# Normalised rows kept in natural order in place of h, h rebuilt from them, two weight pieces asked for in another order

## The chip, the cores and the metric

One core of one Trainium2 chip. The metric is the device time of one execution of the kernel in microseconds (us), the median of several runs. Engines: TensorE (PE), VectorE (DVE), ScalarE (ACT), GpSimd (POOL) and SyncE (SP), which here only asks for DMA transfers.

## The reference

One encoder block over 512 tokens of width 1024, in f32. The parts that matter here:

```
h = h + concat([a, s]) @ w_out              # a: pooling mixer, s: state-space mixer
v = rmsnorm(h, g_ffn)
h = h + hierarchical_moe(v)                 # 4 groups x 8 experts; top-1 group, top-2 experts in it
gate = sigmoid(rmsnorm(h, g_ple) @ ple_gate_w + ple_gate_b)
h = h + gate * (p @ ple_proj_w)
out = rmsnorm(h, g_final)

# expert e, on its tokens: (silu(v @ w_gate[e]) * (v @ w_up[e])) @ w_down[e]
# w_gate, w_up: (1024, 256), w_down: (256, 1024): 3 MB an expert, 96 MB in all
```

Each token's result is the sum of two experts' rows with weights w1 and w2. A row's normalisation is a division by root = sqrt(mean(h^2) + eps), followed by the gain g_ffn on the columns.

## The kernel before

Each engine has a program of its own, written out by hand, and the engines meet at semaphores. The tokens are four tiles of 128 (t = 0 to 3; NT = 4, NA = 3); tile h holds them in SBUF, tokens on partitions, 1024 columns a tile.

Stages, in order: the mixers (to some 165 us); w_out's second half (wout1, eight blocks of 512 columns, on TensorE) whose results VectorE adds into h (residual); the norm and the router (165 to 219 us); 32 experts (to some 447 us); the tail, that is the combination, the gate, and the final norm.

The norm and the router. ScalarE takes the squares of a tile of h with their sum (mean_root) and the root; VectorE inverts the root in place (norm, column S_RS2); ScalarE's scaled_rows multiplies h by it and writes zbuf. It does that in another column order: chunk j of a row (128 columns) gets the columns 8p + j, since w_gate and w_up are loaded with row 8p + j on partition p. TensorE transposes h itself for the router (turned), and VectorE and TensorE make the logits. GpSimd stores each tile of h to h_d and each tile of zbuf to v_d in DRAM. For the first expert pair nothing is gathered: TensorE picks the rows of experts 0 and 1 out of zbuf by matmuls with 0/1 matrices (picked, two groups of tiles: 0 and 1, then 2 and 3, once VectorE's mask of the last tile is there).

The experts. Slots are 64 tokens an expert; for each later pair GpSimd gathers 128 rows of v_d into moe (rows_in), TensorE transposes them in 8 chunks (x_rows, line 1935), VectorE applies the gain and writes them back (x_out). For each expert TensorE does gate and up (32 passes of 256 columns, gate_up), a transpose (h_rows, line 1954), and down (8 passes of 512 columns). ScalarE copies the result out, GpSimd scatters it to pairs_d.

Weights come in pieces of 1 MB: piece p = 3e + k is gate, up or down (k = 0, 1, 2) of expert e. 22 buffers hold them: 12 in ring (0 to 11), 4 in big (12 to 15), 2 in zbuf (16, 17), 2 in h (18, 19), 2 in ut (20, 21). SP asks for the first 22 in an order written by hand, each group behind the wait that says that its buffer is free; from piece 22 on each takes the buffer of piece AFTER[p] once the experts have used it (gu_ps counts gate_up, dn_ps down). So h must be stored before its buffers take pieces 18 and 19, and it is loaded back before the tail (line 498).

The tail. VectorE adds to each tile of h the two gathered rows of pairs_d times the weights S_W1 and S_W2 (combine), then the last two experts' share from a PSUM bank.

Every matmul here goes through L1586, every recorded tensor_tensor of VectorE through L855, every activation copy through L531, every weight request through L356.

Of the kernel before, what the change touches and what calls it, by code (L numbers as in the profile page):

```python
# [26 lines left out]
ALU = mybir.AluOpType  # L27
# [5 lines left out]
P = 128  # L33
# [100 lines left out]
def build(nc, A, out):  # L134
    ctx = ExitStack()
    with ctx:
# [6 lines left out]
        def scratch(name, shape, dt=F32):  # L143
# [32 lines left out]
        S_SS, S_RS, S_EPS, S_W1, S_W2, S_SS2, S_RS2, S_SS3, S_RS3, S_SS4, S_RS4, S_HALF, S_WARM = (  # L176
            0, 4, 8, 12, 16, 20, 24, 28, 32, 36, 40, 44, 45)
        S_A2, S_T1, S_T2 = 64, 64 + 4 * G, 64 + 6 * G
        S_S30 = S_A2
# [45 lines left out]
        v_d = scratch("v_d", [T, DM])  # L225
        h_d = scratch("h_d", [T, DM])
        tbl_d = scratch("tbl_d", [T * NE, 1], I32)
# [9 lines left out]
        down_ready = [sem(f"down_ready{k}") for k in range(LOADS)]  # L237
        h_stored, h_back = sem("h_stored"), sem("h_back")
        half_in, x1_done = sem("half_in"), sem("x1_done")
# [125 lines left out]
        def _(sp):  # L365
# [82 lines left out]
            for p in range(6, 12):  # L448
                weights(sp, p)
            sp.wait_ge(wo1_ps, 2 * NT)  # L450
            for p in (14, 15, 21):
                weights(sp, p)
            sp.wait_ge(turned_ps, KC + 1 + NT)
            sp.wait_ge(h_stored, 16 * NT)
            sp.wait_ge(v_done, NT)
            for p in (18, 19):
                weights(sp, p)
            sp.wait_ge(v_stored, 16 * NT)
            sp.wait_ge(xT_ps, 2)
            for p in (16, 17):  # L460
                weights(sp, p)
# [30 lines left out]
            def load_pairs(t):  # L492
# [5 lines left out]
            sp.dma_start(at(h, ALL, 0, [[DM, NT], [1, DM]]),  # L498
                         dr(h_d, 0, [[DM, P], [P * DM, NT], [1, DM]])).then_inc(h_back, 16)
            sp.wait_ge(gu_ps, NE - 1)  # L500
# [27 lines left out]
        def _(act):  # L528
# [188 lines left out]
            def scaled_rows(t):  # L717

                act.wait_ge(rstd_done, NT + t + 1)
                act.activation(at(zbuf, ALL, t * DM, [[1, P], [P, KC]]), at(h, ALL, t * DM, [[KC, P], [1, KC]]),  # L720
                               ACT.Copy, scale=at(small, ALL, S_RS2 + t, [[1, 1]])).then_inc(v_done, 1)

            for t in range(NA):
                act.wait_ge(h_done, 2 * (t + 1))
                mean_root(at(h, ALL, t * DM, [[1, DM]]), at(zbuf, ALL, t * DM, [[1, DM]]), S_SS2, t, ss_done)
                act.wait_ge(ss_done, NT + t + 1)
                act.activation(at(small, ALL, S_RS2 + t, [[1, 1]]), at(small, ALL, S_SS2 + t, [[1, 1]]), ACT.Sqrt,
                               bias=at(small, ALL, S_EPS, [[1, 1]]), scale=1.0 / DM).then_inc(rms_root, 1)
                scaled_rows(t)
            t = NA  # L730
            act.wait_ge(h_done, 2 * NT - 1)
            mean_root(at(h, ALL, t * DM, [[1, 512]]), at(zbuf, ALL, t * DM, [[1, 512]]), S_HALF, 0, half_in)
            act.wait_ge(h_done, 2 * NT)
            mean_root(at(h, ALL, t * DM + 512, [[1, 512]]), at(zbuf, ALL, t * DM + 512, [[1, 512]]), S_SS2, t, ss_done)
            act.wait_ge(ss_done, 2 * NT)
            act.wait_ge(half_root, 1)
            act.activation(at(small, ALL, S_RS2 + t, [[1, 1]]), at(small, ALL, S_SS2 + t, [[1, 1]]), ACT.Sqrt,
                           bias=at(small, ALL, S_HALF, [[1, 1]]), scale=1.0 / DM).then_inc(rms_root, 1)
# [112 lines left out]
        def _(dve):  # L851
# [211 lines left out]
            def norm(t):  # L1063
                inverse(S_RS2 + t, 1, NT + 1 + t)

# [214 lines left out]
            def weights_and_slots():  # L1280
# [6 lines left out]
                seq(tt(at(small, ALL, S_W1, one), qv("gp", one), qv("dn", one), ALU.mult))  # L1287
                seq(tt(at(small, ALL, S_W2, one), at(small, ALL, S_W1, one), qv("ex", one), ALU.mult))
                for i, x in enumerate((NE - 2, NE - 1)):
                    for k, col in ((1, S_W1), (2, S_W2)):  # L1290
                        own.do(tt(qv("wb", one, (k - 1) * NT), qv(f"M{k}", [[NE, NT]], x), at(small, ALL, col, one), ALU.mult))
                    own.settle()
                    own.do(tt(qv("wt", one, i * NT), qv("wb", one), qv("wb", one, NT), ALU.add))
                    seq(pick(qv(f"X{x}", [[P, NT], [1, P]]), cv(C_PLACE, [[0, NT], [1, P]]), 1.0,
                             qv(f"rk{x}", [[1, NT], [0, P]]), ALU.add, ALU.is_equal))
                    tt(qv(f"X{x}", [[P, NT], [1, P]]), qv(f"X{x}", [[P, NT], [1, P]]), qv("wt", [[1, NT], [0, P]], i * NT),
                       ALU.mult).then_inc(x1_done, 1)
# [33 lines left out]
            def combine(t):  # L1331
                dve.wait_ge(ld_pairs[t], 16)
                if t == 0:
                    dve.wait_ge(h_back, 16)
                for n in range(2):
                    hv = at(h, ALL, t * DM + n * 512, [[1, 512]])
                    for k, col in enumerate((S_W1, S_W2)):
                        dve.scalar_tensor_tensor(hv, at(big, ALL, t * 2 * DM + k * DM + n * 512, [[1, 512]]),
                                                 at(small, ALL, col + t, [[1, 1]]), hv, ALU.mult, ALU.add
                                                 ).then_inc(comb, 1)  # L1340
                        if k == 0:
                            dve.wait_ge(comb, 6 * t + 2 * n + 1)
                for n in range(2):
                    hv = at(h, ALL, t * DM + n * 512, [[1, 512]])
                    dve.wait_ge(cmb_ps, 2 * t + n + 1)
                    dve.wait_ge(comb, 6 * t + 4)
                    tt(hv, bank[2 * t + n][:, :], hv, ALU.add).then_inc(comb, 1)

# [59 lines left out]
        def _(pool):  # L1408
# [82 lines left out]
            for t in range(NT):  # L1491
                pool.wait_ge(h_done, 2 * (t + 1))
                pool.dma_start(dr(h_d, t * P * DM, [[DM, P], [1, DM]]), at(h, ALL, t * DM, [[1, DM]])
                               ).then_inc(h_stored, 16)
                pool.wait_ge(v_done, t + 1)
                pool.dma_start(dr(v_d, t * P * DM, [[DM, P], [1, DM]]), at(zbuf, ALL, t * DM, [[1, DM]])
                               ).then_inc(v_stored, 16)
# [86 lines left out]
        def _(pe):  # L1584
# [270 lines left out]
            def picked(t):  # L1855
# [3 lines left out]
                for j in range(KC):  # L1859
                    got = mm(bank[j // 4 * 6][:, (j % 4) * P:(j % 4 + 1) * P], at(zbuf, ALL, t * DM + j * P, [[1, P]]),  # L1860
                             at(moe, ALL, Q["X1"] + t * P, [[1, P]]), t == 0 and j % 4 == 0, t == NA, True)
# [71 lines left out]
            def x_rows(k):  # L1933
                for j in range(KC):
                    last = pe.transpose(bank[j // 4 * 6][:, (j % 4) * P:(j % 4 + 1) * P],  # L1935
                                        at(moe, ALL, M_XG + k * DM + j * P, [[1, P]]), ident)
                    if j % 4 == 3:
# [151 lines left out]
```

## Time and profile before

| what | value |
|---|---|
| median of 3 runs | 523.9 us (522.33 to 526.2) |
| span of the profiled execution | 522.6 us |
| the profiled execution's own time | the page gives the span alone |
| TensorE busy | 484.2 us (93%) |
| VectorE, ScalarE, GpSimd busy | 238.9, 163.6, 161.0 us |
| HBM read, written | 138.17 MB, 16.29 MB |
| chain that ended last | PE 70%, DMA 18%, DVE 3%, ACT 3%, SP's queue 3% |

The shares of busy time are averages over stages with different limits; the chain and the stretches say what limits which stage. Times in rows are us from the start of the span, unless marked ns.

### The profile page before, as it was taken

The numbers are of one execution on the slowest core, as the hardware profiler recorded it, in microseconds if no ns is written. First come the engines' busy times: TensorE is split into PE (matmuls) and PEld (weight loads), VectorE is DVE, ScalarE is ACT, GpSimd is POOL, SyncE is SP. The second block draws the span as 40 slices with busy tenths as digits, with TensorE's granted clock in tenths as the row PEclk, the third lists the DMA queues.
The fourth block names the chain that finished last, engine by engine and source line by source line (L and its number), as shares of the span: only waits on it lengthen the run. The fifth ranks groups of instructions, "written<-read, shape, count | busy, mean of one in ns | idle before, by whom it ended". The sixth has DMA issues, their size and how long they took to land.

```text
span 522.6 us, 7298 instructions
## 1 busy us (share of the span) xinstructions
PE 484.2 (93%) x2744; PEld 273.3 (52%) x2744; DVE 238.9 (46%) x683; ACT 163.6 (31%) x265; POOL 161.0 (31%) x144
## 2 busy tenths in 40 slices
PE   3799999999999998999999999779999998899993
PEld 3446776634854476765555554435454544444441
DVE  2899987999233347653222222102211211474524
ACT  5643335456442344111111111002212121313464
POOL 1069999944100111132222222202120210003350
PEclk9999999999999989999999999879999998999998
DMA  8874200499289965999999999999999997970012
GB/s 298 141 204 88 62 0 2 159 129 208 108 360 422 415 249 192 407 412 423 418 415 419 417 419 409 423 416 421 418 420 420 419 409 296 345 312 0 0 80 80
DMA packets 57083, 146.83 MB, mean 281 GB/s; under 512 B 27602, under 2 KB 32758, under 8 KB 44248
## 3 DMA queue, kind: packets, MB, share of 16 engines
q1 hardware_dynamic: 50872, 133.92, 69.0%
q0 software_dynamic: 5904, 12.41, 6.1%
q8 instruction: 22, 0.36, 0.3%
q14 instruction: 13, 0.11, 0.1%
q10 hardware_dynamic: 272, 0.04, 0.0%
HBM read 138.17 MB, written 16.29 MB: 296 GB/s over the span
## 4 chain that ended last, share of the span: by engine, by line
PE 70%; DMA 18%; DVE 3%; ACT 3%; SPq 3%; issue 1%; DVEq 0%
PE bank L1586 65%; DMA h<-in_exp_w_up_dram 11%; DMA big<-in_exp_w_up_dram 6%; SPq L356 3%; DMA h<-in_x_dram 1%; PE bank L1935 1%; PE bank L1677 1%; PE bank L1954 1%; ACT L539 1%; ACT moe L531 1%; PE bank L1821 1%; PE bank L2052 1%; DVE ring L855 1%; DVE moe L1092 1%; DVE moe L855 1%
## 5 line engine op out<-in xcount | busy, mean ns | idle before, releaser
L1586 PE MATMUL bank<-ring,moe 128*64 128x256 f32 (+3 forms) x976 | 127.3, 385 | 3.4 <-DMA ring<-in_exp_w_up_dram 3.0
L1586 PEld LDWEIGHTS bank<-ring,moe 128*64 128x64 f32 (+1 forms) x976 | 76.2, 144 | 38.2 <-issue 15.3
L1512 POOL DMA_INDIRECT pairs_d<-moe,sidx_all x32 | 32.0, 1000 | 159.8 <-PE bank L1935 83.0
L855 DVE TENSOR_TENSOR vrow<-moe,bank 64x128 f32<-64x128 f32 x64 | 18.6, 291 | 125.5 <-ACT moe L754 120.6
L1586 PE MATMUL bank<-big,ut 128*128 128x512 f32 x128 | 58.2, 609 | 1.2 <-ACT ut L676 1.2
L1586 PE MATMUL bank<-ut,big 128*128 128x512 f32 x128 | 57.3, 596 | 1.8 <-ACT ut L543 1.8
L754 ACT ACTIVATE moe<-bank 64x256 f32<-64x256 f32 x32 | 12.1, 378 | 143.3 <-PE bank L1586 143.3
L1586 PE MATMUL bank<-ring,ut 128*128 128x512 f32 x128 | 55.7, 593 | 0.4 <-DVE ut L855 0.4
L531 ACT ACTIVATE moe<-bank 128x512 f32<-128x512 f32 x56 | 32.6, 598 | 59.8 <-PE bank L1586 49.3
L1586 PE MATMUL bank<-big,moe 128*64 128x256 f32 (+1 forms) x264 | 44.9, 455 | 6.6 <-DMA big<-in_exp_w_up_dram 5.7
L1586 PEld LDWEIGHTS bank<-big,ut 128*128 128x128 f32 x128 | 24.6, 196 | 32.0 <-issue 31.7
L855 DVE TENSOR_TENSOR ring<-ring,bank 128x64 f32<-128x64 f32 (+1 forms) x142 | 39.5, 278 | 2.8
L1586 PEld LDWEIGHTS bank<-ring,ut 128*128 128x128 f32 x128 | 24.0, 190 | 29.3 <-issue 29.3
L1586 PEld LDWEIGHTS bank<-ut,big 128*128 128x128 f32 x128 | 23.4, 190 | 27.2 <-issue 26.6
L855 DVE TENSOR_TENSOR bank<-bank,ring 128x64 f32<-128x64 f32 (+1 forms) x142 | 35.2, 288 | 2.9
L1586 PEld LDWEIGHTS bank<-big,moe 128*64 128x64 f32 x264 | 22.5, 148 | 22.3 <-issue 7.6
L1586 PE MATMUL bank<-ring 128*64 128x128 f32 (+1 forms) x128 | 32.5, 437 | 0.0
L1272 DVE COPY moe<-bank 128x128 f32<-128x128 f32 x32 | 9.3, 292 | 44.9 <-PE bank L1954 44.8
L855 DVE TENSOR_TENSOR moe<-bank,vec 128x512 f32<-128x512 f32 x40 | 26.0, 687 | 5.5 <-PE bank L1935 3.5
L1580 POOL TENSOR_TENSOR ring<-ring,zbuf 128x512 f32<-128x512 f32 x6 | 8.7, 1444 | 47.7 <-ACT ring L816 47.7
L1586 PE MATMUL bank<-h,moe 128*64 128x256 f32 (+1 forms) x120 | 19.5, 454 | 4.1 <-DMA h<-in_exp_w_up_dram 4.1
L1586 PEld LDWEIGHTS bank<-ring 128*64 128x64 f32 (+1 forms) x128 | 15.2, 163 | 15.3 <-issue 15.0
(193 smaller groups left out, 600.5 us busy)
## 6 DMA issues: line engine op xcount, KB each, us to landing
ring<-in_exp_w_up_dram SPq DMA_DIRECT2D x19, 1024.0 KB
ring<-in_exp_w_down_dram SPq DMA_DIRECT2D x18, 1024.0 KB
ring<-in_exp_w_gate_dram SPq DMA_DIRECT2D x17, 1024.0 KB
big<-in_exp_w_gate_dram SPq DMA_DIRECT2D x7, 1024.0 KB
big<-in_exp_w_down_dram SPq DMA_DIRECT2D x7, 1024.0 KB
big<-in_exp_w_up_dram SPq DMA_DIRECT2D x6, 1024.0 KB
ut<-in_exp_w_gate_dram SPq DMA_DIRECT2D x4, 1024.0 KB
h<-in_exp_w_up_dram SPq DMA_DIRECT2D x4, 1024.0 KB
```

The costliest lines, as they stand in the source:

```text
L356: eng.dma_start(at(to[0], ALL, to[1], [[1, PIECE]]), w[e].rearrange("(p j) f -> p (j f)", p=P)).then_inc(done, 16)
L531: act.activation(o, i, ACT.Copy).then_inc(signal, 1)
L539: act.activation(at(small, ALL, S_WARM + k, [[1, 1]]), at(small, ALL, S_EPS, [[1, 1]]), function)
L754: act.activation(at(moe, (0, CAP), M_SG, [[1, DE]]), at(bank[1 + e % 2], (0, CAP), 0, [[1, DE]]), ACT.Silu).then_inc(sg_sb, 1)
L855: return dve.tensor_tensor(o, a, b, op)
L1092: return dve.scalar_tensor_tensor(o, a, b, c, op0, op1)
L1272: dve.tensor_copy(at(moe, ALL, M_HT + (e % 2) * P, [[1, P]]), bank[3][:, 0:P]).then_inc(hT_sb, 1)
L1512: pool.indirect_dma_start(pairs, bass.IndirectOffsetOnAxis(ap=index, axis=0), at(moe, ALL, M_Y + k * 512, [[1, 512]]), None, bounds_check= ...
L1580: seq(pool.tensor_tensor(sg, sg, at(zbuf, ALL, n * 512, [[1, 512]]), ALU.mult))
L1586: return pe.matmul(o, a, b, start=start, stop=stop, skip_group_check=loose)
L1677: last = pe.transpose(bank[B_WT + ri][:, (g % 4) * P:(g % 4 + 1) * P], rv(R_W + ri * 1024 + g * P, P), ident)
L1821: rows = pe.transpose(bank[H_BANK[t] + n][:, (j % 4) * P:(j % 4 + 1) * P], at(h, ALL, t * DM + j * P, [[1, P]]), ident)
```

## The change

The normalised rows are no longer written to zbuf but over h, in natural column order. TensorE then reads them with a step: the picks take columns j, j + 8, j + 16 ... of h, and x_rows does the same with the gathered rows. ScalarE therefore waits, ahead of each scaling, until TensorE has transposed that tile of h. h is not stored; the reload at line 498 takes v_d, and the combination works in normalised units: the roots are kept in S_ROOT2 beside the inverses, two new products S_V hold w1 and w2 times the inverse, and the last step of a tile multiplies by the root while it adds the bank. The squares' unused output goes to moe. SP asks for pieces 16 and 17 (zbuf) straight behind the ring's; 18 and 19 (h) take the place at which 16 and 17 stood, behind v_stored and xT_ps (the last pick).

```diff
--- before.py
+++ after.py
@@ -175,6 +175,7 @@
 
         S_SS, S_RS, S_EPS, S_W1, S_W2, S_SS2, S_RS2, S_SS3, S_RS3, S_SS4, S_RS4, S_HALF, S_WARM = (
             0, 4, 8, 12, 16, 20, 24, 28, 32, 36, 40, 44, 45)
+        S_ROOT2, S_V = 52, 56
         S_A2, S_T1, S_T2 = 64, 64 + 4 * G, 64 + 6 * G
         S_S30 = S_A2
 
@@ -223,7 +224,6 @@
         z_d = scratch("z_d", [P, G * NCH])
         k_d = scratch("k_d", [G * CH, 15 * CH])
         v_d = scratch("v_d", [T, DM])
-        h_d = scratch("h_d", [T, DM])
         tbl_d = scratch("tbl_d", [T * NE, 1], I32)
         pairs_d = scratch("pairs_d", [4 * T, DM // 2])
 
@@ -235,7 +235,7 @@
             sem(n) for n in ("ld_wout0", "ld_wlow", "ld_wout1", "ld_glu", "ld_ppw", "ld_wple", "ld_fin"))
         gu_ready = [sem(f"gu_ready{k}") for k in range(LOADS)]
         down_ready = [sem(f"down_ready{k}") for k in range(LOADS)]
-        h_stored, h_back = sem("h_stored"), sem("h_back")
+        h_back, vw_done = sem("h_back"), sem("vw_done")
         half_in, x1_done = sem("half_in"), sem("x1_done")
         cmb_ps = sem("cmb_ps")
         dve_step, pool_step = sem("dve_step"), sem("pool_step")
@@ -447,17 +447,14 @@
             sp.wait_ge(cat_done, NB)
             for p in range(6, 12):
                 weights(sp, p)
+            for p in (16, 17):
+                weights(sp, p)
             sp.wait_ge(wo1_ps, 2 * NT)
             for p in (14, 15, 21):
                 weights(sp, p)
-            sp.wait_ge(turned_ps, KC + 1 + NT)
-            sp.wait_ge(h_stored, 16 * NT)
-            sp.wait_ge(v_done, NT)
-            for p in (18, 19):
-                weights(sp, p)
             sp.wait_ge(v_stored, 16 * NT)
             sp.wait_ge(xT_ps, 2)
-            for p in (16, 17):
+            for p in (18, 19):
                 weights(sp, p)
             for p in range(NPIECE, 3 * NE):
                 e, k = AFTER[p] // 3, AFTER[p] % 3
@@ -496,7 +493,7 @@
 
             sp.wait_ge(gu_ps, NE - 5)
             sp.dma_start(at(h, ALL, 0, [[DM, NT], [1, DM]]),
-                         dr(h_d, 0, [[DM, P], [P * DM, NT], [1, DM]])).then_inc(h_back, 16)
+                         dr(v_d, 0, [[DM, P], [P * DM, NT], [1, DM]])).then_inc(h_back, 16)
             sp.wait_ge(gu_ps, NE - 1)
             load_gate(0, 0, 4, ld_wple)
             sp.wait_ge(moe_done, 1)
@@ -717,24 +714,25 @@
             def scaled_rows(t):
 
                 act.wait_ge(rstd_done, NT + t + 1)
-                act.activation(at(zbuf, ALL, t * DM, [[1, P], [P, KC]]), at(h, ALL, t * DM, [[KC, P], [1, KC]]),
-                               ACT.Copy, scale=at(small, ALL, S_RS2 + t, [[1, 1]])).then_inc(v_done, 1)
+                act.wait_ge(turned_ps, KC + t + 1 + (t == NA))
+                hv = at(h, ALL, t * DM, [[1, DM]])
+                act.activation(hv, hv, ACT.Copy, scale=at(small, ALL, S_RS2 + t, [[1, 1]])).then_inc(v_done, 1)
 
             for t in range(NA):
                 act.wait_ge(h_done, 2 * (t + 1))
-                mean_root(at(h, ALL, t * DM, [[1, DM]]), at(zbuf, ALL, t * DM, [[1, DM]]), S_SS2, t, ss_done)
+                mean_root(at(h, ALL, t * DM, [[1, DM]]), at(moe, ALL, M_XT, [[1, DM]]), S_SS2, t, ss_done)
                 act.wait_ge(ss_done, NT + t + 1)
-                act.activation(at(small, ALL, S_RS2 + t, [[1, 1]]), at(small, ALL, S_SS2 + t, [[1, 1]]), ACT.Sqrt,
+                act.activation(at(small, ALL, S_ROOT2 + t, [[1, 1]]), at(small, ALL, S_SS2 + t, [[1, 1]]), ACT.Sqrt,
                                bias=at(small, ALL, S_EPS, [[1, 1]]), scale=1.0 / DM).then_inc(rms_root, 1)
                 scaled_rows(t)
             t = NA
             act.wait_ge(h_done, 2 * NT - 1)
-            mean_root(at(h, ALL, t * DM, [[1, 512]]), at(zbuf, ALL, t * DM, [[1, 512]]), S_HALF, 0, half_in)
+            mean_root(at(h, ALL, t * DM, [[1, 512]]), at(moe, ALL, M_XT, [[1, 512]]), S_HALF, 0, half_in)
             act.wait_ge(h_done, 2 * NT)
-            mean_root(at(h, ALL, t * DM + 512, [[1, 512]]), at(zbuf, ALL, t * DM + 512, [[1, 512]]), S_SS2, t, ss_done)
+            mean_root(at(h, ALL, t * DM + 512, [[1, 512]]), at(moe, ALL, M_XT + 512, [[1, 512]]), S_SS2, t, ss_done)
             act.wait_ge(ss_done, 2 * NT)
             act.wait_ge(half_root, 1)
-            act.activation(at(small, ALL, S_RS2 + t, [[1, 1]]), at(small, ALL, S_SS2 + t, [[1, 1]]), ACT.Sqrt,
+            act.activation(at(small, ALL, S_ROOT2 + t, [[1, 1]]), at(small, ALL, S_SS2 + t, [[1, 1]]), ACT.Sqrt,
                            bias=at(small, ALL, S_HALF, [[1, 1]]), scale=1.0 / DM).then_inc(rms_root, 1)
             scaled_rows(t)
 
@@ -1061,7 +1059,10 @@
                 tt(hv, bank[n][:, :], hv, ALU.add).then_inc(h_done, 1)
 
             def norm(t):
-                inverse(S_RS2 + t, 1, NT + 1 + t)
+                dve.wait_ge(rms_root, NT + 1 + t)
+                dve.reciprocal(at(small, ALL, S_RS2 + t, [[1, 1]]), at(small, ALL, S_ROOT2 + t, [[1, 1]])
+                               ).then_inc(rstd_done, 1)
+                dve.wait_ge(rstd_done, NT + 1 + t)
 
             def turned(t):
 
@@ -1286,6 +1287,9 @@
                 seq(dve.reciprocal(qv("dn", one), qv("dn", one)))
                 seq(tt(at(small, ALL, S_W1, one), qv("gp", one), qv("dn", one), ALU.mult))
                 seq(tt(at(small, ALL, S_W2, one), at(small, ALL, S_W1, one), qv("ex", one), ALU.mult))
+                for k, col in enumerate((S_W1, S_W2)):
+                    tt(at(small, ALL, S_V + k * NT, one), at(small, ALL, col, one), at(small, ALL, S_RS2, one), ALU.mult
+                       ).then_inc(vw_done, 1)
                 for i, x in enumerate((NE - 2, NE - 1)):
                     for k, col in ((1, S_W1), (2, S_W2)):
                         own.do(tt(qv("wb", one, (k - 1) * NT), qv(f"M{k}", [[NE, NT]], x), at(small, ALL, col, one), ALU.mult))
@@ -1332,9 +1336,10 @@
                 dve.wait_ge(ld_pairs[t], 16)
                 if t == 0:
                     dve.wait_ge(h_back, 16)
+                    dve.wait_ge(vw_done, 2)
                 for n in range(2):
                     hv = at(h, ALL, t * DM + n * 512, [[1, 512]])
-                    for k, col in enumerate((S_W1, S_W2)):
+                    for k, col in enumerate((S_V, S_V + NT)):
                         dve.scalar_tensor_tensor(hv, at(big, ALL, t * 2 * DM + k * DM + n * 512, [[1, 512]]),
                                                  at(small, ALL, col + t, [[1, 1]]), hv, ALU.mult, ALU.add
                                                  ).then_inc(comb, 1)
@@ -1344,7 +1349,8 @@
                     hv = at(h, ALL, t * DM + n * 512, [[1, 512]])
                     dve.wait_ge(cmb_ps, 2 * t + n + 1)
                     dve.wait_ge(comb, 6 * t + 4)
-                    tt(hv, bank[2 * t + n][:, :], hv, ALU.add).then_inc(comb, 1)
+                    dve.scalar_tensor_tensor(hv, hv, at(small, ALL, S_ROOT2 + t, [[1, 1]]), bank[2 * t + n][:, :],
+                                             ALU.mult, ALU.add).then_inc(comb, 1)
 
             def turned_g_ple(t):
                 for n in range(2):
@@ -1489,11 +1495,8 @@
             pool.wait_ge(wo0_done, 2 * NT)
 
             for t in range(NT):
-                pool.wait_ge(h_done, 2 * (t + 1))
-                pool.dma_start(dr(h_d, t * P * DM, [[DM, P], [1, DM]]), at(h, ALL, t * DM, [[1, DM]])
-                               ).then_inc(h_stored, 16)
                 pool.wait_ge(v_done, t + 1)
-                pool.dma_start(dr(v_d, t * P * DM, [[DM, P], [1, DM]]), at(zbuf, ALL, t * DM, [[1, DM]])
+                pool.dma_start(dr(v_d, t * P * DM, [[DM, P], [1, DM]]), at(h, ALL, t * DM, [[1, DM]])
                                ).then_inc(v_stored, 16)
             pool.wait_ge(log_ps, NT)
             own.do(pool.memset(at(moe, ALL, M_XG + DM, [[1, DM]]), 0.0))
@@ -1857,7 +1860,7 @@
                 pe.wait_ge(x1_done, 1 if t < NA else 2)
                 pe.wait_ge(v_done, t + 1)
                 for j in range(KC):
-                    got = mm(bank[j // 4 * 6][:, (j % 4) * P:(j % 4 + 1) * P], at(zbuf, ALL, t * DM + j * P, [[1, P]]),
+                    got = mm(bank[j // 4 * 6][:, (j % 4) * P:(j % 4 + 1) * P], at(h, ALL, t * DM + j, [[KC, P]]),
                              at(moe, ALL, Q["X1"] + t * P, [[1, P]]), t == 0 and j % 4 == 0, t == NA, True)
                     if t == NA and j % 4 == 3:
                         got.then_inc(xT_ps, 1)
@@ -1933,7 +1936,7 @@
             def x_rows(k):
                 for j in range(KC):
                     last = pe.transpose(bank[j // 4 * 6][:, (j % 4) * P:(j % 4 + 1) * P],
-                                        at(moe, ALL, M_XG + k * DM + j * P, [[1, P]]), ident)
+                                        at(moe, ALL, M_XG + k * DM + j, [[KC, P]]), ident)
                     if j % 4 == 3:
                         last.then_inc(xT_ps, 1)
 
```

## Rows read from the trace of the kernel before

**Rows 1.** The profile's page: the span.

```profile
span 522.6 us, 7298 instructions
```

**Rows 2.** Stretches: busy us (x instructions) by engine, granted clock, DMA share, GB/s.

```profile
core 0: us, PE busy (x) PEld busy (x) DVE busy (x) ACT busy (x) POOL busy (x), PEclk, DMA share, GB/s
...
185.00:200.70 15.70, 15.70 (x83) 10.83 (x82) 9.49 (x38) 6.12 (x7) 1.59 (x3) 0.89 0.38 153
...
219.20:226.00 6.80, 5.74 (x42) 3.08 (x43) 5.55 (x21) 0.74 (x2) 2.77 (x3) 1.00 1.01 419
...
234.10:322.00 87.90, 87.83 (x659) 49.08 (x661) 22.83 (x59) 14.27 (x29) 22.77 (x23) 1.00 1.02 417
322.00:437.70 115.70, 102.40 (x648) 52.47 (x644) 19.96 (x54) 20.03 (x39) 19.77 (x20) 0.96 1.01 416
```

**Rows 3.** TensorE's waits between 300 and 450: us in total, times, longest.

```profile
PE bank L1586 <- DMA big<-in_exp_w_up_dram: 5.7, 2, 3.4
PE bank L1586 <- DMA h<-in_exp_w_up_dram: 4.1, 2, 3.4
```

**Rows 4.** The chain that ended last, 400 to 450: start us, us, what.

```profile
405.13 0.87 PE bank L1935 x8
...
406.37 31.25 DMA big<-in_exp_w_up_dram
...
437.66 7.01 PE bank L1586 x40
```

**Rows 5.** SP's timeline, first ask of each group: start us, us, what.

```profile
200.68 0.33 SPq L356 DMA_DIRECT2D big<-in_exp_w_down_dram  x1
...
211.52 0.33 SPq L356 DMA_DIRECT2D h<-in_exp_w_gate_dram  x1
...
214.15 0.33 SPq L356 DMA_DIRECT2D zbuf<-in_exp_w_up_dram  x1
...
219.18 0.33 SPq L356 DMA_DIRECT2D ring<-in_exp_w_up_dram  x1
...
225.95 0.33 SPq L356 DMA_DIRECT2D ring<-in_exp_w_gate_dram  x1
...
234.10 0.33 SPq L356 DMA_DIRECT2D ring<-in_exp_w_gate_dram  x1
```

**Rows 6.** The DMA queues between 200.6 and 226; GB/s in 40 slices of 0.635 us.

```profile
GB/s 0 103 155 374 374 387 284 284 303 348 355 426 432 400 394 452 426 439 400 374 323 374 400 400 400 400 413 413 452 400 426 413 439 426 426 406 419 400 445 413
...
q1 hardware_dynamic: 1106, 8.14, 81.2%
q0 software_dynamic: 411, 1.29, 12.5%
```

**Rows 7.** Groups of ScalarE by form: busy us, mean ns, idle before.

```profile
L720 ACT ACTIVATE zbuf<-h,small 128x1024 f32<-128x1024 f32 x4 | 8.3, 2083 | 11.8 <-DVE small L866 11.8
...
L535 ACT ACTIVATE zbuf<-h 128x1024 f32<-128x1024 f32 x3 | 3.2, 1053 | 5.4 <-DVE h L855 5.4
```

**Rows 8.** TensorE's timeline, 176 to 229: start us, us, what, idle before.

```profile
178.00 7.03 PE L1586 MATMUL bank<-big,ut 128*128 128x512 f32 x16
...
209.02 0.63 PE L1586 MATMUL bank<-moe,cst 128*128 128x32 f32 x4 [1.36 <-DVE moe L1092]
209.49 3.82 PE L1586 MATMUL bank<-moe,zbuf 128*128 128x128 f32 x32
```

**Rows 9.** VectorE's timeline: start us, us, what, idle before.

```profile
149.35 1.41 DVE L1050 SCALAR_TENSOR_TENSOR ring<-zbuf,vec,bank 128x512 f32<-128x512 f32 x2 [3.08 <-PE bank L1789]
...
222.05 0.23 DVE L855 TENSOR_TENSOR moe<-moe,small 128x4 f32<-128x4 f32 x2
...
453.61 1.29 DVE L855 TENSOR_TENSOR h<-bank,h 128x512 f32<-128x512 f32 x2
```

**Rows 10.** TensorE's operand loads by form: busy us, mean ns, idle before.

```profile
L1586 PEld LDWEIGHTS bank<-ring,moe 128*64 128x64 f32 x848 | 61.5, 137 | 37.2 <-issue 14.3 <-DMA ring<-in_exp_w_up_dram 3.5
...
L1935 PEld LDWEIGHTS bank<-cst,moe 128*128 128x128 f32 x120 | 13.4, 140 | 0.8 <-DMA moe<-v_d,gidx_all 0.8
...
L1586 PEld LDWEIGHTS bank<-rw,moe 128*128 128x128 f32 x64 | 7.4, 192 | 0.1
```

## The prediction

> **What bounds the kernel now.** First the span, 522.6 us [rows 1]. Then the stretches [rows 2]: between 185.0 and 200.7 us the DMA engines are busy for 0.38 of the time, and from 219.2 to 437.7 us for all of it, at 417 GB/s. TensorE is never idle in a way that matters before 322 us (87.83 of 87.90 us busy), but between 322 and 437.7 it works 102.40 of 115.70 us. So the experts have two phases: at first TensorE sets the pace and weights are ahead of it, later it has used up that lead and takes each weight as it lands. The waits [rows 3] say for what: weights, 5.7 us for those in big and 4.1 us for those in h alone. The chain that ended last [rows 4] shows the end of it: the last up-weights are asked for at 406.37, land at 437.66, and only then does the last expert start. A change in this kernel is therefore worth what it does to the landing of the last weights: when the DMA engines had nothing to move, and how much they must move in all. TensorE work is cheap as long as it fits into the 13.3 us (115.70 - 102.40) in which it waits.
>
> What can be asked for when is SP's list [rows 5]: three pieces at 200.68, the two pieces of h at 211.52 (line 454, behind the stores of h), the two pieces of zbuf at 214.15, when the picked rows are out of zbuf, two more at 219.18, three at 225.95, three at 234.10; each of the later ones waits until an expert has used its buffer.
>
> **The early pieces.** The change asks for the two zbuf pieces behind the ring's, that is at about 168 us. They then move while the DMA engines are two thirds idle: 2 x 1.0486 MB at 417 GB/s is 5.0 us, and the gap is 15.7 x (1 - 0.38) = 9.7 us wide. Nothing waits behind them on SP's queue but the wait for wout1. The fourth store of h (0.52 MB, 1.3 us), which lies in the busy stretch, goes too; the three before it lay in the gap and cost nothing. Naively the last weights would land 5.0 + 1.3 = 6.3 us sooner.
>
> **What is given back.** The pieces of h must now wait until the picked rows are out of h, as zbuf's did: 214.15 instead of 211.52. The three pieces of 200.68 (3.15 MB, 7.5 us) and the last store of rows (0.52 MB, 1.3 us) are moved by about 210.5 us, so the queue is empty for some 4.5 us before 215.2 (the first bytes come about 1.0 us after an ask, as the first slices of the queue's view show: 0 and 103 GB/s [rows 6]). Now the count that matters, at 226.0. Before: 9 pieces, 9.44 MB, were asked for since 200.6 and 8.14 MB of them moved [rows 6] (the tenth, of 225.95, has hardly begun), so 1.30 MB, 3.1 us, were outstanding. After: from 215.2 the pieces of h and those of 219.18, 4.19 MB, and the gathers' 0.24 MB (1.29 - 1.05 of queue 0, the 1.05 being the two stores of 0.52 MB each [rows 6]) take 4.43 / 0.417 = 10.6 us, to 225.8. The queue is then just empty, and the pieces of 225.95 begin at about 227.0. The lead is 3.1 us and 1.0 us of it is lost to that start: 2.1 us. It can't be more, since no buffer is free sooner; between 227.0 and 235.1 three pieces and queue 0's share (3.15 + about 0.3 MB) fill 8.1 us x 0.417 = 3.4 MB, so no further gap opens. From there the DMA engines are full to the end, as before, and the lead reaches the last landing. Its bounds: 3.1 us if the start is hidden, 1 us if the slowest of the 16 engines, which decides a landing, was emptier than the mean. I take 2.3 us, a little over the count, since part of the gathers' bytes moves after 226.
>
> **Small terms.** ScalarE's scaling of the rows takes 2083 ns with both sides stepped and should take what a contiguous pass over h takes, 1053 ns [rows 7]: 1.0 us less, four times. None of it is on the path: the last two picks wait for VectorE's mask (1.36 us idle before 209.02 [rows 8]). ScalarE's new wait for TensorE's transposes costs nothing by the order on TensorE, where the transposes of a tile precede its scaling in all four tiles; behind it stand only ScalarE's next squares and root. If that cover were missing, the last tile would carry it to the picks, less than 1 us. VectorE gets two products of 4 columns between the weights and the slot matrices: two such take 0.23 us [rows 9] at 222 us, where a delay only releases buffers 0.1 to 0.2 us later. In the tail the add of bank and h becomes a multiply and add of the same operands: 1.29 us for two adds against 1.41 us for two instructions of that kind that read a bank [rows 9], so 0.12 us a tile, of which one or two tiles lie on the path. The reload of h moves the same 2 MB. Together 0.3 us lost at most.
>
> **The stepped reads.** TensorE now reads h and the gathered rows with a step of 8 elements, 32 bytes, always as the operand that it loads: in the 120 transposes of gathered rows (15 groups of 8, 0.87 us each [rows 4]) and in the 64 passes of the picks (3.82 us for 32 [rows 8]). No row shows a stepped operand on TensorE, so I bound it. A load of 128 columns takes 192 ns in a matmul, one of 64 takes 137, so a column costs 0.86 ns and the rest is a fixed 82; in a transpose 128 columns take 140 ns [rows 10], 0.45 ns each. The pace of the transposes, 0.87 / 8 = 109 ns, is then that of the other operand's 128 columns (16 passes of 512 columns in 7.03 us [rows 8], 0.86 ns a column), not of the load. So the read of a loaded operand can run at 0.45 ns, and if a step halves that rate, it is 0.9: the transposes stay at 109 to 116 ns and the picks at 119. That is the lower bound, 0 to 0.8 us in all. A gain is excluded, the same columns are loaded. The middle is a doubling of the picks' 0.86, to 1.7 ns: 213 ns a load, +104 x 120 = 12.5 us for the transposes, and +3.2 us for each 32 passes of the picks, of which 1.36 us were idle: 5.0 us. The upper bound is what ScalarE pays, 2.03 ns an element (2083 / 1024) [rows 7]: 260 ns a load, 18.1 us for the transposes and 4.5 us for each 32 passes, 7.6 us with the idle time taken off. I take the lower bound, since the row nearest to it is of the same engine and the same operand.
>
> The Trainium skill has a rule that speaks against the change (Advanced Engine Details and Errata, SBUF Cachelines): a line of SBUF is 16 bytes, and with a different line for each access there is a penalty. ScalarE's rows agree, 2083 against 1053 ns [rows 7]; that it reaches TensorE's loads no row shows. If it doubles their time, the result is that of the second case below, if the load hides it, that of the first.
>
> **The cases.** The profiled span is 522.6 us, 1.3 us under the median of the three runs, and the page gives no other time of that execution; I apply the differences to the median, 523.9. A measurement of this kernel can tell about 1%, 5.2 us, from no change.
> 1. The forecast: loads hide the steps, lead 2.3 us: 521.6. Chance 0.50.
> 2. Slower: the steps double the loads. The ask for the h pieces and the release of every later buffer come 5.0 us later, and the lead of 2.1 us pays a part: +3 us. TensorE's own sum, 12.5 + 5.0 = 17.5 us, just fits into its 13.3 us of waits and the 0.04 x 115.7 = 4.6 us that the lowered clock costs it between 322 and 437.7 [rows 2]; I add 0.3: 527.2. It decides as soon as each group of picks grows by more than 1.5 us. For it: ScalarE's stepped rows. Against: the transposes' loads, twice as fast as they need be. Chance 0.28.
> 3. Slower still: the loads cost what ScalarE pays. 18.1 + 7.6 = 25.7 us against 17.9: TensorE sets the end, +8, 532. Chance 0.07.
> 4. The naive sum counts in full, the queue doesn't run dry: -6.3 us, 517.6. Against it: buffers are released only at 219 and 226 us. Chance 0.07.
> 5. The removed stores and early pieces only shift the gap: 523.9. Chance 0.08.
>
> The range takes in cases 1, 2 and 5 with their bounds, 518.2 to 528.2, and leaves out 3 and 4 (0.14). Faster by over 1% (under 518.7): case 4 and a corner of 1, 0.09. Slower by over 1% (over 529.1): case 3 and the upper end of 2, 0.11. Within: 0.80.
>
> **What would show it.** The DMA share between 185 and 200.7 rises from 0.38 to about 0.7. A new gap stands between about 210.5 and 215.2, and the queue is thin at 226. The groups of eight stepped transposes take 0.87 us and the 32 passes 3.82: this tells cases 1, 2 and 3 apart at a glance. TensorE's waits between 322 and 437 stay near 13 us; the last up-weights land at about 435.4, and from there to the end it is 84.9 us as before. The prediction is wrong if the picks grow, if the queue is dry for more than about 1 us after 219, or if the tail changes length, for instance because the clock falls elsewhere: the last expert's 7.01 us [rows 4] stand in a stretch whose granted clock is below full.

## The result and the profile after

The changed kernel takes 528.11 us (median of 4, 527.24 to 530.38) against 524.52 us for the kernel before on the same chip: ratio 1.0087, 95% interval 1.0052 to 1.0123. By the ratio that is 4.6 us more (2.7 to 6.5), where 2.3 us less was forecast. The profiled execution took 530.38 us, its span is 528.3 us, 5.7 us over the span before [rows 1].

The prediction named the rows to look at first: the picks (the matmuls that take the rows of experts 0 and 1 out of h) and the transposes of the gathered rows. TensorE's timeline of the changed kernel (start us, us, what):

```profile
178.53 7.03 PE L1589 MATMUL bank<-big,ut 128*128 128x512 f32 x16
...
204.37 7.86 PE L1589 MATMUL bank<-moe,h 128*128 128x128 f32 x32
212.06 0.53 PE L1589 MATMUL bank<-moe,cst 128*128 128x32 f32 x4
212.43 7.86 PE L1589 MATMUL bank<-moe,h 128*128 128x128 f32 x32
```

The first row is where it was, 0.53 us later. SP's asks at 144.14 and 144.67 us already differ by as much, so this part of the difference between the two spans arose before anything that was changed, and it is taken off below. Each group of 32 passes takes 7.86 us in place of 3.82 [rows 8], and no idle time is left between the groups. TensorE's loads by form follow: those of the picks in the kernel before, then those of the picks and of the transposes in the changed kernel. The last fence has rows of the chain that ended last (400 to 460 us).

```profile
L1586 PEld LDWEIGHTS bank<-moe,zbuf 128*128 128x128 f32 x64 | 7.3, 192 | 0.0
```

```profile
L1589 PEld LDWEIGHTS bank<-moe,h 128*128 128x128 f32 x64 | 15.4, 335 | 0.0
...
L1938 PEld LDWEIGHTS bank<-cst,moe 128*128 128x128 f32 x120 | 14.5, 190 | 0.7 <-DMA moe<-v_d,gidx_all 0.7
```

```profile
411.89 0.89 PE bank L1938 x8
...
412.93 30.32 DMA big<-in_exp_w_up_dram
...
443.30 7.08 PE bank L1589 x40
```

```profile
168.71 1.07 SPq L356 DMA_DIRECT2D zbuf<-in_exp_w_up_dram  x1
...
201.20 0.33 SPq L356 DMA_DIRECT2D big<-in_exp_w_down_dram  x1
...
220.39 0.33 SPq L356 DMA_DIRECT2D h<-in_exp_w_gate_dram  x1
...
226.16 0.33 SPq L356 DMA_DIRECT2D ring<-in_exp_w_up_dram  x1
...
232.93 0.33 SPq L356 DMA_DIRECT2D ring<-in_exp_w_gate_dram  x1
```

```profile
185.00:200.70 15.70, 15.70 (x82) 11.00 (x81) 9.03 (x34) 4.35 (x7) 1.08 (x2) 0.89 0.48 197
...
214.20:219.20 5.00, 5.00 (x23) 5.00 (x22) 1.35 (x4) 0.92 (x2) 0.00 (x0) 1.00 0.00 0
...
322.00:437.70 115.70, 105.17 (x680) 55.26 (x678) 21.25 (x56) 19.99 (x39) 20.85 (x21) 0.97 1.01 418
```

```profile
232.90:322.00 89.10, 88.43 (x663) 50.68 (x665) 24.31 (x67) 14.90 (x31) 24.16 (x25) 1.00 1.01 409
```

The zbuf pieces are early, as the change says. The h pieces are asked for at 220.39, while the kernel before reached the same place in the list at 214.15 [rows 5], and between 214.2 and 219.2 the DMA engines move nothing. The row of queue 1 between 200.6 and 232.9 us (packets, MB, share) says how the queue stands when the next three pieces are asked for:

```profile
q1 hardware_dynamic: 963, 7.10, 58.8%
```

Seven pieces, 7.34 MB, were asked for and 7.10 moved: 0.24 MB are left, where the kernel before had 1.30 MB at 226.0. The sum: that point comes 232.9 - 226.0 - 0.5 = 6.4 us later, and 1.06 MB more have moved by then, 2.5 us of work at 417 GB/s. That leaves 3.9 us. The last up-weights land 443.30 - 437.66 - 0.53 = 5.1 us later, so another 1.2 us were lost behind that point. The prediction put about 1.0 us on the start of the next pieces into an empty queue; the rate behind it is lower, 409 GB/s from 232.9 to 322 against 417 [rows 2], but how the 1.2 us divide is not shown. From the landing to the end it is 85.0 us, before 84.9.

### The profile page after: what moved, and what is told of

Read it like the earlier page. It is cut to its first block, busy times and chain, and to the rows that moved or that the text cites. A ratio compares the mean times of both kernels' runs of the same rounds, so it can differ in the third digit from the quotient of the medians.

```text
span 528.3 us, 7299 instructions
## 1 busy us (share of the span) xinstructions
PE 491.6 (93%) x2744; PEld 281.5 (53%) x2744; DVE 238.6 (45%) x685; ACT 159.9 (30%) x265; POOL 157.7 (30%) x140
## 4 chain that ended last, share of the span: by engine, by line
PE 71%; DMA 20%; ACT 3%; DVE 2%; SPq 2%; issue 1%; DVEq 0%; POOL 0%; POOLq 0%
PE bank L1589 66%; DMA big<-in_exp_w_up_dram 6%; DMA h<-in_exp_w_up_dram 6%; DMA ring<-in_exp_w_up_dram 5%; DMA moe<-v_d,gidx_all 2%; SPq L356 2%; PE bank L1938 1%; DMA h<-in_x_dram 1%; PE bank L1680 1%; ACT moe L528 1%; PE bank L1957 1%; ACT L536 1%; PE bank L1824 1%; PE bank L2055 1%; DVE moe L853 0%
## 5 line engine op out<-in xcount | busy, mean ns | idle before, releaser
L1589 PE MATMUL bank<-ut,big 128*128 128x512 f32 x128 | 59.1, 611 | 2.6 <-ACT ut L540 2.6
L1510 POOL DMA_INDIRECT moe<-v_d,gidx_all x15 | 15.6, 1042 | 23.5 <-DVE sidx_all L1242 18.8
L528 ACT ACTIVATE zbuf<-bank 128x512 f32<-128x512 f32 x16 | 11.5, 717 | 36.5 <-PE bank L1589 36.5
```

The lines of the kernel that those rows point to most:

```text
L528: act.activation(o, i, ACT.Copy).then_inc(signal, 1)
L1510: pool.indirect_dma_start(at(moe, ALL, M_XG + k * DM, [[1, DM]]), None, v_d, bass.IndirectOffsetOnAxis(ap=index, axis=0), bounds_check=T - ...
L1589: return pe.matmul(o, a, b, start=start, stop=stop, skip_group_check=loose)
```

## The experiments

In all of them ratios are to the kernel before, run on the same chip. Where experts compute on the wrong columns, the text under Expected says so: those kernels measure time and are no replacement.

**Picks without a step** (the changed kernel):

```
-  mm(..., at(h, ALL, t * DM + j, [[KC, P]]), at(moe, ALL, Q["X1"] + t * P, ...
+  mm(..., at(h, ALL, t * DM + j * P, [[1, P]]), at(moe, ALL, Q["X1"] + t * P, ...
```

> The changed kernel, with one thing altered: the picks read 128 adjacent columns of h instead of every eighth, so experts 0 and 1 compute on the wrong columns. Theory 1, the stepped loads of the picks are the whole loss: 32 passes take 3.8 us again instead of 7.9, the h pieces are asked for at about 214.5 instead of 220.4, and the time is 2 us below the kernel before (ratio 0.996), that is some 5 us below the changed kernel. Theory 2, the loss lies elsewhere (tail, gathers, order of the asks): the ratio stays between 1.005 and 1.012.

Measured 521.14 us, ratio 0.9962 (0.9945 to 0.9978). Its timeline and chain:

```profile
202.55 3.82 PE L1589 MATMUL bank<-moe,h 128*128 128x128 f32 x32
207.25 3.82 PE L1589 MATMUL bank<-moe,h 128*128 128x128 f32 x32
```

```profile
402.13 31.91 DMA big<-in_exp_w_up_dram
434.08 5.39 PE bank L1589 x40
```

The picks are back at 3.82 us and the whole loss is gone: the kernel is 2.0 us (1.2 to 2.9) faster than the one before. The second theory is out: the tail, the gathers and the list of asks cost too little together to cancel that gain. This is close to the 2.3 us that the prediction forecast with unslowed picks; the section on why it was wrong says by which route.

**Zbuf pieces late** (the changed kernel):

```
-  for p in (16, 17): weights(sp, p)        # behind the ring's
...
-  for p in (18, 19):
+  for p in (18, 19, 16, 17):
```

> The changed kernel, but the two zbuf pieces are asked for where the kernel before asked for them, behind the h pieces. Theory 1, the DMA engines have run dry by the time of the next asks at 233, so the early pieces save what the late ones would keep them busy with: the last up-weights land 5.0 us later less the 1 us of the dry spell that they fill, time 4 us above the changed kernel, ratio to the kernel before 1.016. Theory 2, early pieces are worth nothing because buffers set the pace: the time of the changed kernel, 1.008.

Measured 532.89 us, ratio 1.0172 (1.0144 to 1.0200): 0.85% or 4.5 us over the changed kernel's ratio, where 4 us were expected. The two intervals don't meet, so the early asks are worth something; by their widths the 4.5 us are good to some 2.3 us (an estimate), and the two traces say 3.1 (table below). In this kernel, without them the loss would have been larger, by the ratios about twice as large.

**Stepped picks in the kernel before:**

```
-  mm(..., at(zbuf, ALL, t * DM + j * P, [[1, P]]), ...
+  mm(..., at(zbuf, ALL, t * DM + j, [[KC, P]]), ...
```

> The kernel before, with one thing altered: the picks read every eighth column of zbuf, so experts 0 and 1 compute on the wrong columns. Theory 1: 32 passes take 7.9 us, zbuf pieces and every later buffer come 6.4 us later, while the h pieces are still asked for at 211.5; the DMA engines run dry for about 3 us before 221 and have no backlog at 233, as in the changed kernel, so the time is as much above the kernel before as the changed kernel's or a little more: ratio 1.009. Theory 2, the step matters only through h: 1.000 to 1.003.

Measured 529.14 us, ratio 1.0121 (1.0095 to 1.0146). The stretch in which the DMA engines starve:

```profile
215.00:221.00 6.00, 5.87 (x37) 4.89 (x36) 2.66 (x5) 0.00 (x0) 0.00 (x0) 1.00 0.63 233
```

The step alone, with everything else as before, costs 6.3 us (5.0 to 7.6), as much as the whole change or more (the intervals overlap, so which of the two is more stays open). The h pieces don't wait for the picks in this kernel and were asked for at 209.87. That didn't prevent the loss: the zbuf pieces and every later buffer still wait for the picks.

**The price by the size of the step.** The changed kernel with picks that read every second, third and fourth column; one execution each:

```
-  at(h, ALL, t * DM + j, [[KC, P]])
+  at(h, ALL, t * DM + j % 4 * P, [[2, P]])     # or 3, or 4
```

> The changed kernel, but the picks read every second column (8 bytes) of 256, so experts 0 and 1 compute on the wrong columns. Theory 1, a line of 16 bytes counts and two hits in a line are enough: 32 passes take 3.8 us, a load 192 ns. Theory 2, any step doubles a load: 7.9 us and 335 ns.

> The changed kernel, but the picks read every third column (12 bytes), so experts 0 and 1 compute on the wrong columns. Theory 1, a line of 16 bytes counts: 128 columns touch 96 lines, so the price is between: 32 passes take about 5.2 to 7.9 us. Theory 2, the price starts at 16 bytes: 3.8 us.

> The changed kernel, but the picks read every fourth column (16 bytes), so experts 0 and 1 compute on the wrong columns. Theory 1, one hit in a line: 32 passes take 7.9 us and a load 335 ns, as with a step of 8. Theory 2, the price grows with the distance: less than that.

The picks of the three, in that order, each its second group, and the mean of a load:

```profile
208.64 4.01 PE L1589 MATMUL bank<-moe,h 128*128 128x128 f32 x32
...
L1589 PEld LDWEIGHTS bank<-moe,h 128*128 128x128 f32 x64 | 7.7, 196 | 0.0
```

```profile
207.74 5.79 PE L1589 MATMUL bank<-moe,h 128*128 128x128 f32 x32
...
L1589 PEld LDWEIGHTS bank<-moe,h 128*128 128x128 f32 x64 | 11.3, 261 | 0.0
```

```profile
209.66 7.71 PE L1589 MATMUL bank<-moe,h 128*128 128x128 f32 x32
...
L1589 PEld LDWEIGHTS bank<-moe,h 128*128 128x128 f32 x64 | 15.1, 329 | 0.0
```

With steps of 1, 2, 3, 4 and 8 a group of 32 passes takes 3.82, 4.01, 5.79, 7.71 and 7.86 us. A step of two is nearly free, a step of four costs the full price, and eight costs no more than four. These executions took 522.56, 525.02 and 526.94 us beside 522.65 for the kernel before. The order is that of the picks, but they are single executions, and those of one kernel lie up to 4 us apart, so the price of a step is read from the passes and not from these times.

The Trainium skill has a rule (Advanced Engine Details and Errata, SBUF Cachelines): a line of 16 bytes, and at least two hits in it to hide the access. The traces agree with it on TensorE's loads too. At a step of two f32 every line gets two reads, 4.01 us; at four and eight each gets one, 7.71 and 7.86. At a step of three, 12 bytes, two of every four reads share a line and two are alone, so half of the price is due: 3.82 + (7.71 - 3.82) / 2 = 5.8 us, an estimate from that rule and the two rows; 5.79 was measured.

**Transposes without a step** (the changed kernel, picks still stepped):

```
-  at(moe, ALL, M_XG + k * DM + j, [[KC, P]]), ident)
+  at(moe, ALL, M_XG + k * DM + j * P, [[1, P]]), ident)
```

> The changed kernel, with one thing altered: the transposes of the gathered rows read 128 adjacent columns, so experts 2 to 31 compute on the wrong columns; the picks stay stepped. Theory 1, the transposes hide their slower loads behind the identity's stream and what little they cost lies in TensorE's waits: the time of the changed kernel within 0.5 us, ratio to the kernel before 1.008 to 1.010. Theory 2, their loads (190 ns in place of 140) cost 0.05 us each after all, 6 us in all: ratio 0.998 to 1.002.

Measured 529.06 us, ratio 1.0116 (1.0095 to 1.0136), not below the changed kernel's 1.0087 (1.0052 to 1.0123), and its loads take 141 ns. So the 120 stepped transposes cost nothing that can be measured: theory 1, though the ratio is above the window it gave, and the 0.998 to 1.002 of theory 2 is out. That they are paced by the identity's 128 columns, as the prediction had it, fits their 0.89 / 8 = 111 ns against 128 x 0.86 = 110; no run varied the identity.

**The kernel before without stores of h:**

```
-  pool.dma_start(dr(h_d, ...), at(h, ...)).then_inc(h_stored, 16)      # and the wait for it
-  dr(h_d, 0, ...)).then_inc(h_back, 16)
+  dr(v_d, 0, ...)).then_inc(h_back, 16)
```

> The kernel before without the four stores of h and without the wait for them; what is loaded back is the scaled rows, so the output misses h. Theory 1: of the four stores only the last lies in the busy stretch, so 0.52 MB fewer are moved there and the last weights land 1.3 us sooner: ratio 0.9975. Theory 2, buffers bound the asks and the queue is shorter at 226 but not empty: the same 1.3 us, no more, although the h pieces are asked for 5 us sooner. Theory 3, stores of GpSimd's queue cost nothing beside weights: 1.000.

Measured 521.99 us, ratio 0.9986 (0.9968 to 1.0005). The expected 0.9975 and no effect both lie in the interval, so this doesn't settle what a store is worth. The h pieces were asked for at 205.47 instead of 211.52, and even so the stores and these earlier asks together are worth 1.7 us at most: an ask put behind pieces that still keep the queue busy gained nothing that shows here.

**Plain picks by another layout of four pieces.** The loss can be avoided in a kernel that computes the right result. Only experts 0 and 1 are picked, and their gate and up weights can be loaded with the rows in natural order, so that their tokens are wanted in adjacent columns:

```
+  if natural:      # gate and up of experts 0 and 1
+      eng.dma_start(at(to[0], ALL, to[1], [[DE, KC], [1, DE]]),
+                    w[e].rearrange("(j p) f -> p j f", p=P)).then_inc(done, 16)
-  x_out(0, xT_sb, 2)
+  x_out(0, xT_sb, 2, V_FB)                      # g_ffn in natural chunks
-  at(h, ALL, t * DM + j, [[KC, P]])
+  at(h, ALL, t * DM + j * P, [[1, P]])
```

> The changed kernel without the stepped picks, by another layout for the two experts that are picked: gate and up of experts 0 and 1 are loaded with row 128 j + p on partition p, in runs of 1 KB in place of 8 KB, the picks read adjacent columns, and the gain of that pair is taken in the other order. It computes the reference. Theory 1: as with plain picks alone, 2 us below the kernel before, ratio 0.996, if the four pieces in 1 KB runs land by the first expert; their transfer lies between 145 and 165 us, and if it is slower it only fills the gap after 190. Theory 2, short runs are so slow that the ring's pieces are late: expert 0 waits for weights and the ratio is over 1.005.

Measured 521.50 us, ratio 0.9968 (0.9952 to 0.9984): 1.7 us faster than the kernel before and 6.2 us faster than the changed one, and every expert reads the right columns. Two of its stretches:

```profile
143.00:166.00 23.00, 23.00 (x99) 11.41 (x96) 7.86 (x9) 8.84 (x13) 1.27 (x1) 1.00 0.95 334
...
186.00:201.00 15.00, 15.00 (x91) 11.00 (x91) 10.52 (x38) 5.36 (x10) 1.08 (x2) 1.00 0.59 233
```

The four pieces in runs of 1 KB lie in the first stretch, and it is slower: 334 GB/s against 373 in the kernel before between 143 and 166 us. What is late by it only fills the gap behind (share 0.59 from 186 to 201, 0.33 before), and TensorE waits for none of it.

**And the first two tiles of h released early,** on top of that:

```
-  sp.wait_ge(v_stored, 16 * NT); sp.wait_ge(xT_ps, 2); weights(sp, 18); weights(sp, 19)
+  sp.wait_ge(v_first, 32); sp.wait_ge(x_zero, 2); weights(sp, 18)     # tiles 0 and 1 stored and picked
+  sp.wait_ge(v_stored, 32); sp.wait_ge(xT_ps, 2); weights(sp, 19)
```

> The kernel with plain picks and the other layout for experts 0 and 1, and piece 18 (tiles 0 and 1 of h) asked for as soon as the first two tiles are picked and stored, at about 208, piece 19 where it was. Theory 1, buffers bound the lead: the queue is empty at 226 either way, and the gap before 215 is only exchanged for one between 222 and 227; gain over the kernel without this 0 to 0.5 us, ratio to the kernel before 0.996. Theory 2, the gap counts in full: 2.5 us sooner, ratio 0.992.

Measured 521.94 us, ratio 0.9981 (0.9967 to 0.9995). Its stretches around the asks:

```profile
208.00:215.00 7.00, 6.85 (x58) 6.02 (x59) 5.32 (x21) 1.80 (x4) 0.00 (x0) 1.00 0.93 344
215.00:221.00 6.00, 4.88 (x43) 3.40 (x44) 2.51 (x13) 0.38 (x1) 2.29 (x3) 1.00 0.65 249
```

The gap before 215 is filled (share 0.93, without this 0.59) and stands after it instead (0.65, without this 0.95). No gain, as the first theory had it.

**All the traces, measured from the first pick.** The early part of a trace is up to 2.8 us shorter or longer, mostly with TensorE's clock (last section). From the start of the first pick to the start of the last expert's matmuls, which wait for the last up-weights, that part is left out (starts in us, from TensorE's timelines):

| kernel | first pick | last expert | between |
|---|---|---|---|
| before | 203.84 | 437.66 | 233.8 |
| before, stepped picks | 202.45 | 441.57 | 239.1 |
| before, no stores of h | 203.48 | 436.50 | 233.0 |
| changed | 204.37 | 443.30 | 238.9 |
| changed, zbuf pieces late | 204.58 | 446.59 | 242.0 |
| changed, plain transposes | 204.13 | 443.62 | 239.5 |
| changed, picks of step 4, 3, 2 | 201.75, 201.75, 203.94 | 440.55, 437.91, 436.18 | 238.8, 236.2, 232.2 |
| changed, plain picks | 202.55 | 434.08 | 231.5 |
| plain picks, other layout | 202.15 | 433.76 | 231.6 |
| the same, h released early | 203.85 | 436.43 | 232.6 |

These are single traces, but they agree with the ratios: with stepped picks of 8 both kernels are 5.1 to 5.3 us behind the kernel before, and with plain picks the change gains 2.2 to 2.3.

## Why the prediction was wrong

**What bounds the kernel** was right: the landing of the last weights, set by when the DMA engines ran dry. From the last up-weights to the end the changed kernel is as long as the one before, and TensorE's extra work in the transposes is free. TensorE works 105.17 of the 115.7 us between 322 and 437.7, so it still waits 10.5 us there, where about 13 were forecast.

**The lead** was right in size: 2.1 us were counted and 2.3 taken, and with plain picks the kernel gains 2.0 us (1.2 to 2.9). The naive sum of 6.3 us (case 4) and "only shifts the gap" (case 5) are both out. The DMA share between 185 and 200.7 was forecast at 0.7 and is 0.48. Two things had been left out of that sentence, though not out of the sum: the stores of h that went (queue 0 moved 1.51 MB there, before 2.37), and that a part of the two zbuf pieces moves before 185 (they are 2.10 MB, and queue 1 moved 1.57 in the stretch).

The route was in part another one, so that the size came out so well is in part luck. The prediction says of ScalarE's shorter scaling "None of it is on the path: the last two picks wait for VectorE's mask". But the mask, which says whose rows are picked, came sooner with the shorter scaling. The rows, first of the kernel before, then of the changed one: ScalarE's last scaling, GpSimd's memset behind it, and one comparison of VectorE among the steps to the mask. The last row is TensorE's wait for the mask with plain picks.

```profile
203.65 2.10 ACT L720 ACTIVATE zbuf<-h,small 128x1024 f32<-128x1024 f32 x1 [1.18 <-DVE small L866]
...
206.25 1.32 DVE L1187 TENSOR_SCALAR moe<-moe 128x8 f32<-128x8 f32 x1
...
206.56 0.97 POOL L1499 MEMSET moe<- 128x1024 f32 x1
```

```profile
204.18 1.15 ACT L719 ACTIVATE h<-h,small 128x1024 f32<-128x1024 f32 x1 [1.19 <-DVE small L1063]
...
206.14 0.97 POOL L1502 MEMSET moe<- 128x1024 f32 x1
...
206.77 0.37 DVE L1188 TENSOR_SCALAR moe<-moe 128x8 f32<-128x8 f32 x1
```

```profile
206.78 0.63 PE L1589 MATMUL bank<-moe,cst 128*128 128x32 f32 x4 [0.41 <-DVE moe L1093]
```

GpSimd clears a part of moe as soon as it has asked for the store of the last scaled rows. In all twelve traces this comparison ends 0.03 to 0.04 us after that memset, whether it takes 1.32 us or 0.36. The kernel has no wait between the two; that GpSimd's memset holds VectorE up is what the rows point to, and no run moved it. With the scaling 0.95 us shorter the mask comes 0.95 us sooner, TensorE's idle time before the last picks falls from 1.36 to 0.41 us, and every release behind them comes 0.95 us sooner. At the ask that corresponds to 226.0, 223.7 us with plain picks, 0.40 MB were then still outstanding (7 pieces less 6.94 MB), where the prediction had counted an empty queue. So of the 2.3 us between the traces 0.95 come from the earlier releases and 1.3 from the queue.

**The step that failed** is "I take the lower bound, since the row nearest to it is of the same engine and the same operand". It took the load of a transpose, 0.45 ns a column, for what the read path can do, and concluded that a step, which halves that rate to 0.9 ns a column, would be hidden in a matmul pass too. The runs showed instead that a step of 8 about doubles each kind of load from its own base: 0.45 to 0.84 ns a column in the transposes ((190 - 82) / 128), 0.86 to 1.98 in the picks ((335 - 82) / 128). These are estimates with the prediction's fixed 82 ns, which no run checked with a step. The first is hidden, as said; the second is not. Plain picks in the changed kernel and stepped picks in the one before show it from both sides. The picks grew by 4.04 us for 32 passes, between the doubling (3.2) and what ScalarE pays (4.5), and 2 x 4.04 less the 1.36 us of idle time is 6.7 us. SP's list shows 5.7 of them at the ask for the h pieces (220.39 - 214.15 - 0.53) and 6.4 at the two releases behind it (226.16 - 219.18 - 0.53).

**Case 2** is what happened, in its mechanism and nearly in its size: 5.0 us later asks and +3 us were its terms, measured 6.4 at the next release and +4.6 us by the ratio (2.7 to 6.5). Its second half, transposes that add 12.5 us to TensorE, did not happen. The row that spoke for it, ScalarE's 2083 against 1053 ns [rows 7], and the rule beside it were the right guide, and weighed too little against a guess on what a load of another kind leaves free. A slip in the sums doesn't change this: case 2 counts the 0.3 us of small terms and case 1, 521.6, leaves them out.

**The small terms** came out near what was worked out, apart from the path of the scaling: it takes 1149 ns for 1053 forecast, the tail's multiply and add 1.41 us for two, the two products 0.23 us. ScalarE's new wait is named in 10.8 us of its idle time, but the scalings start within 0.15 us of where they stood before, since ScalarE was idle there anyway. The lines:

```profile
L719 ACT ACTIVATE h<-h,small 128x1024 f32<-128x1024 f32 x4 | 4.6, 1149 | 13.5 <-PE bank L1824 10.8 <-DVE small L1063 2.7
```

```profile
229.03 0.23 DVE L853 TENSOR_TENSOR small<-small 128x4 f32<-128x4 f32 x2
...
459.23 1.41 DVE L1352 SCALAR_TENSOR_TENSOR h<-h,small,bank 128x512 f32<-128x512 f32 x2
```

## What to carry to other kernels

A stepped read costs in full where the operand that it slows paces the instruction (the picks, 3.82 to 7.86 us), and nothing where the other operand does (the transposes). So look for each stepped read at which of the two it is. In f32 on TensorE the picks' time about doubled from a step of four on, and each kind of load has to be priced from its own base. Where buffers limit the asks, count the bytes outstanding at the next release, before and after: that, and not the bytes moved into a gap, is what an earlier transfer can gain. Before calling a term off the path, follow what waits behind it on the other engines: here the scaling reached the picks over GpSimd and VectorE. And a layout can be changed for the few pieces that need it, at a time when the queue has room for them.

## What the runs showed of the hardware that wasn't expected

The load of TensorE's operand in f32 takes 192, 196, 261, 329 and 335 ns for 128 columns at steps of 1, 2, 3, 4 and 8, and in a transpose 140 and 190 at 1 and 8. A transpose's load is the faster one at either step; why was not tried.

One comparison of 8 columns on VectorE lasts 1.32 us in some of the traces and 0.36 or 0.37 in the others. In each of the twelve it overlaps a memset of 1024 columns on GpSimd and ends 0.03 to 0.04 us after it.

Single spans carry some noise from TensorE's clock. In the last expert the same 40 passes took 7.01 us in the profiled execution before and 7.08 after, but 5.39 with plain picks. Between 185.0 and 201.2 us the granted clock was 0.89 in the first two and 1.00 in the last: for a part of the stretch the first two ran at the level of 1.2 GHz, the last at that of 2.4 throughout. Such a stretch makes up to 1.7 us, as much as the gains at issue. It touches the medians a little too: the executions with plain picks have a mean granted clock of 0.988, those of the kernel before beside them 0.983, and by a straight line through the latter (1.55 us for 0.01) some 0.7 us of the 2.0 could be the clock's, an estimate. The 2.2 to 2.3 us between the first pick and the last expert don't contain the early stretch. What decides which execution gets the lower level there was not tried.
